# Self attention's queries and keys made block by block in one pipeline with the linear attention's norm

## The chip, the cores and the metric

One core of one Trainium2 chip runs the whole program. The metric is the device time of one execution in microseconds (us), lower is better. Engines: PE (TensorE), DVE (VectorE), ACT (ScalarE), POOL (GpSimd), SP (SyncE, which only issues DMAs here).

## The reference

Two transformer blocks over 1024 tokens of width 1024, batch 1, float32. The change lies in the first third of the first block, its two mixers, which read the same projected input:

```python
h = rms_norm(x, norm_mix)
c_q, c_kv, k_rope, hq, hf_fwd, hf_bwd, hi, hg = split_columns(h @ w_in)   # 192, 128, 32, 5 x 512
# self attention (MLA): 8 heads, q and k 64 + 32 wide, v 64 wide
q = (rms_norm(c_q, q_a_norm) @ w_q_up).reshape(B, S, 8, 96)
kv = (rms_norm(c_kv, kv_a_norm) @ w_kv_up).reshape(B, S, 8, 128)
k = concat([kv[..., :64], broadcast(k_rope)]); v = kv[..., 64:]
q, k = rms_norm(q, q_norm), rms_norm(k, k_norm)         # over 96, each head
q, k = [concat([t[..., :64], apply_rope(t[..., 64:], cos, sin)]) for t in (q, k)]
a = softmax(q @ k.T * 96 ** -0.5) @ v
# linear attention (HGRN2): 4 heads of 128, both directions
o = direction(hf_fwd) + direction(hf_bwd)
r = rms_norm(o, o_norm) * silu(hg)
x = x + concat([a, r]) @ w_out
```

Cross attention and an expert layer end the first block; a state space mixer and an MLP make the second.

## The kernel before

The kernel is written engine by engine. A stage is a `Block` in which each engine has its own instruction list, in the written order; semaphores carry the dependencies, and at the end of a block all engines meet. `c.chain` makes each of an engine's instructions wait for the one before it. Tokens lie in 8 blocks of 128 (`NT`), a block on the 128 partitions.

`mix_first` (L1188) runs the stages of the mixers:

- `norm_split` normalises and transposes the input. In the same block SP fetches small parameters (L1239).
- `project` (L364 to L509) is the product with `w_in`: 6 jobs of 8 weight pieces; for each piece ACT and DVE cut the weights into a high and a low part (L420, L424) and PE makes three products for each of 8 PSUM banks. Three cut pieces can stand ready. ACT evacuates job 0 into `mla_in` (c_q, c_kv, k_rope), job 1 with Silu, jobs 2 and 3 with two Sigmoids a bank.
- `hgrn` is the linear attention; its result goes to `mixed`, half of `mix_hT`.
- `group_norm` (L860 to L866), a product with the gate (L1270) and `turn` (L588) give `r` transposed.
- `mla`: `rope_tables` loads the positions and makes sine and cosine; `load` fetches weights and gains (L170); two `group_norm`s treat c_q and c_kv; a `turn` transposes them with the gains in its evacuation (L1377 to L1382); a block multiplies them up (L1400 to L1428), with PSUM for two token blocks at a time (`mla_up_ps`, 4 banks each); `mla_norms` normalises q and k in 8 parts, ACT squares, DVE sums and scales, POOL applies the gain (L1472 to L1501); `rope` rotates q on DVE and k on POOL (L1512 to L1515); two `turn`s transpose q and k (64 transposes of 96 x 128 each, copied out by ACT L593 and DVE L597).
- `head_pairs` is the attention: 64 units of 128 queries of a head; the row maximum gives the bias of the exponential (L807), whose scale is the constant `96 ** -0.5` (L830).

Each of these stages is its own block, so the stages do not overlap.

Of the kernel before, what the change touches and what calls it, by code (L numbers as in the profile page):

```python
# [17 lines left out]
P = 128  # L18
# [8 lines left out]
T = 1024  # L27
# [692 lines left out]
def head_pairs(c, name, qT, kT, v, room, mixT, scale):  # L720
# [15 lines left out]
    with ExitStack() as ctx:  # L736
# [19 lines left out]
        with nc.Block() as block:  # L756
# [68 lines left out]
            def _(act):  # L825
                def exps(i):
                    act.wait_ge(bias_ready, i + 1)
# [138 lines left out]
def hgrn(c, inputs, q, keep, key, values, lb, lb1, mask, queries, out):  # L966
# [11 lines left out]
    with ExitStack() as ctx:  # L978
        s = lambda n, shape: sbuf(ctx, nc, f"hg_{n}", shape)
        whole = s("whole", [P, 2, 2, T // 2])  # L980
        mine, pairT = s("mine", [P, 2, T]), s("pairT", [P, 2, NT, P])
        kdT, state = s("kdT", [P, 2, NT, P]), s("state", [P, 2, NT, P])
# [203 lines left out]

def mix_first(c, a, x):
    nc = c.nc  # L1188
    with ExitStack() as ctx:
        s = lambda n, shape, dt=F32: sbuf(ctx, nc, n, shape, dt)  # L1190
        hT, high = twins(ctx, nc, "mix_hT", "mix_high", [P, KD, T])
        mla_in = s("mla_in", [P, NT, QR + KVR + ROPE])
        w_in = a["w_in"][0].rearrange("(k p) n -> p k n", p=P)
        with ExitStack() as hg:
            s = lambda n, shape, dt=F32: sbuf(hg, nc, n, shape, dt)
            q = s("hg_q", [P, HH, T])
# [4 lines left out]
            key = s("hg_key", [P, 2, HH, T])  # L1201
# [16 lines left out]
            low = sbuf(low_, nc, "mix_low", [P, KD, T])  # L1218
# [6 lines left out]
            with low_:  # L1225
# [7 lines left out]
                small += [(onorm[:, 0], a["hg_o_norm"][0].unsqueeze(0).to_broadcast([P, HK]))]  # L1233
                small_in = c.hold_sem("hg_parameters_in")
# [10 lines left out]
                project(c, "mix_in", stream, jobs)  # L1245
# [15 lines left out]
            mixed = hT[:, 4:8].rearrange("p k t -> p (k t)").rearrange("p (m v) -> p m v", v=HH * HK)  # L1261
            hgrn(c, a, q, logf, key, values, lb, lb1, mask, queries, mixed)
            ssq = s("hg_ssq", [P, NT * HH])
            heads = lambda t: t.rearrange("p m (h v) -> p (m h) v", v=HK)
            group_norm(c, "hg_norm", heads(mixed), heads(values[:]), ssq[:], HK, onorm[:])
            with nc.Block() as block:
                @block.vector
                def _(dve):
                    do = c.chain("vector", dve)
                    do(nc.vector.tensor_tensor(values[:], mixed, gate[:], ALU.mult))  # L1270
            items = [[values[:, m, h * P:(h + 1) * P] for h in range(HH)] for m in range(NT)]
            turn(c, "hg_turn", items, lambda n, ps, copy: copy(
                hT[:, HH:, n * P:(n + 1) * P], ps.rearrange("p (h t) -> p h t", t=P)))
        mla(c, a, mla_in, hT, x[:].rearrange("p m d -> p (m d)"))
# [29 lines left out]


def rope_tables(c, ctx, a):

    nc = c.nc
    s = lambda n, shape, dt=F32: sbuf(ctx, nc, n, shape, dt)
    cos, sin = s("rope_cos", [P, NT, HALF]), s("rope_sin", [P, NT, HALF])  # L1310
    with ExitStack() as tmp:
        s = lambda n, shape, dt=F32: sbuf(tmp, nc, n, shape, dt)
        wide = a["positions"].dtype != I32
        posi = s("rope_posi", [P, NT, 2 if wide else 1], I32)
        pos, ang, t = s("rope_pos", [P, NT]), s("rope_ang", [P, NT, HALF]), s("rope_tmp", [P, NT, HALF])
        src = a["positions"][0]
        if wide:
            src = src.bitcast(I32)
        load(c, [(posi[:], src.rearrange("(m p two) -> p m two", p=P, two=2 if wide else 1))])
        with nc.Block() as block:  # L1320
            @block.vector
            def _(dve):
                do = c.chain("vector", dve)
                do(nc.vector.tensor_copy(pos[:], posi[:, :, 0]))
                for j in range(HALF):
                    freq = float(np.float32(1.0) / np.float32(ROPE_BASE ** (j / HALF)))
                    do(nc.vector.tensor_scalar(ang[:, :, j], pos[:], freq, None, ALU.mult))
                reduce_angle(nc, do, ang[:], t[:])

                do(nc.vector.tensor_scalar(t[:], ang[:], -1.0, None, ALU.mult))  # L1330
                do(nc.vector.tensor_tensor(t[:], t[:], ang[:], ALU.min))
                do(nc.vector.tensor_scalar(t[:], t[:], math.pi / 2, None, ALU.add))
        with nc.Block() as block:
            @block.scalar
            def _(act):
                nc.scalar.activation(sin[:], ang[:], ACT.Sin)
                nc.scalar.activation(cos[:], t[:], ACT.Sin)
    return cos, sin


def mla(c, a, mla_in, mixT, x):

# [1743 lines left out]
```

## Time and profile before

| | |
|---|---|
| three runs | median 3866.33 us (3858.35 to 3868.52) |
| the profiled execution | 3865.7 us, of it the profile's span 3864.0 us |
| PE busy | 3165.1 us, 82% of the span |
| DVE, ACT, POOL busy | 1470.3 (38%), 898.7 (23%), 175.4 us (5%) |
| mean granted PE clock | 0.904 of full speed |

In the page the span is cut into 40 slices of 96.6 us; the digits are the busy tenths of an engine in a slice, and PEclk the granted clock of PE in tenths (10 is printed as 9). The stages touched here are slices 5 to 7 of the lines below, from some 483 us to 773 us.

```profile
PE   7995732898869696477777279899999889999998
DVE  3116857776251432411111374652122433332334
ACT  3224311444141423000000113102132132111221
POOL 0000004000000000011111030000000000000000
PEclk9997966999989896689899689999999989999999
```

### The profile page before, as it was taken

Reading aid. Unit: us, or ns where it says so; the run is one execution under the profiler, and the core shown is the slowest. Engines: PE = TensorE matmul, PEld = TensorE weight load, DVE = VectorE, ACT = ScalarE, POOL = GpSimd, SP = SyncE. Lnnn points to the kernel's source line nnn. Section 1 sums busy time; section 2 is a strip of 40 time slices with the busy share of each in tenths; the row PEclk is TensorE's granted clock in tenths of the full one; section 3 lists DMA queues with packets and bytes.
Section 4 is the critical chain, followed back from the end, with each engine's and each line's share of the span. In section 5 each row is a group of like instructions: output and inputs, shape, how many; then the busy total and the mean of one; then the engine's idle time right before and its main releaser. Section 6 shows DMA issues by size and latency. Waiting matters only on the chain. (4 is left out here: it accounts for less than half of the span.)

```text
span 3864.0 us, 35977 instructions
## 1 busy us (share of the span) xinstructions
PE 3165.1 (82%) x14454; PEld 2342.5 (61%) x14454; DVE 1470.3 (38%) x2130; ACT 898.7 (23%) x1397; POOL 175.4 (5%) x220
## 2 busy tenths in 40 slices
PE   7995732898869696477777279899999889999998
PEld 7875721544657575222222168788877768888886
DVE  3116857776251432411111374652122433332334
ACT  3224311444141423000000113102132132111221
POOL 0000004000000000011111030000000000000000
PEclk9997966999989896689899689999999989999999
DMA  2110000001121014399999502211111211111111
GB/s 90 49 36 9 1 13 0 1 1 60 63 87 33 12 33 178 121 393 398 398 400 392 185 25 63 58 64 49 41 39 52 82 44 47 47 49 50 49 49 71
DMA packets 138439, 370.35 MB, mean 96 GB/s; under 512 B 44896, under 2 KB 59104, under 8 KB 112160
## 3 DMA queue, kind: packets, MB, share of 16 engines
q1 hardware_dynamic: 129072, 351.45, 25.4%
q0 software_dynamic: 9216, 16.80, 1.2%
q8 instruction: 106, 1.74, 0.2%
q14 instruction: 45, 0.37, 0.0%
HBM read 352.99 MB, written 32.79 MB: 100 GB/s over the span
## 5 line engine op out<-in xcount | busy, mean ns | idle before, releaser
L1873 PE MATMUL moe_ph<-moe_wgu,moe_rowsT 128*64 128x512 f32 x1024 | 264.1, 675 | 82.6 <-DMA moe_wgu<-in_moe_w_up_dram 43.6
L509 PE MATMUL mlp_ps<-mlp_high,mlp_w_cut 128*128 128x512 f32 x1024 | 317.1, 391 | 6.0 <-DVE mlp_w_cut L424 6.0
L509 PE MATMUL mlp_ps<-mlp_w_cut,mlp_hidden_high 128*128 128x512 f32 x1024 | 315.2, 389 | 0.0
L424 DVE TENSOR_TENSOR m_w_cut<-m_w_raw,m_w_cut 128x512 fp32r<-128x512 f32 (+1 forms) x92 | 94.3, 1029 | 453.4 <-ACT m_w_cut L420 453.1
L1873 PEld LDWEIGHTS moe_ph<-moe_wgu,moe_rowsT 128*64 128x64 f32 x1024 | 83.2, 155 | 243.5 <-issue 190.6
L424 DVE TENSOR_TENSOR mlp_w_cut<-mlp_w_raw,mlp_w_cut 128x1024 fp32r<-128x1024 f32 x64 | 78.3, 1225 | 398.9 <-ACT mlp_w_cut L420 398.4
L509 PEld LDWEIGHTS mlp_ps<-mlp_high,mlp_w_cut 128*128 128x128 f32 x1024 | 193.2, 189 | 46.6 <-DVE mlp_w_cut L424 6.4
L420 ACT ACTIVATE m_w_cut<-m_w_raw 128x512 fp32r<-128x512 f32 (+1 forms) x92 | 76.4, 835 | 604.3 <-PE m_gates_ps L509 196.4
L509 PEld LDWEIGHTS mlp_ps<-mlp_w_cut,mlp_hidden_high 128*128 128x128 f32 x1024 | 192.2, 188 | 39.9
L509 PE MATMUL mlp_ps<-mlp_low,mlp_w_cut 128*128 128x512 f32 x512 | 199.9, 390 | 0.0
L509 PE MATMUL mlp_ps<-mlp_w_cut,mlp_hidden_low 128*128 128x512 f32 x512 | 199.2, 389 | 0.0
L420 ACT ACTIVATE mlp_w_cut<-mlp_w_raw 128x1024 fp32r<-128x1024 f32 x64 | 67.6, 1058 | 528.1 <-PE mlp_ps L509 525.6
L509 PE MATMUL m_cv_ps<-m_high,m_w_cut 128*128 128x512 f32 x512 | 166.6, 408 | 25.1 <-DVE m_w_cut L424 15.9
L509 PE MATMUL m_gates_ps<-m_high,m_w_cut 128*128 128x512 f32 x512 | 160.9, 396 | 4.1 <-DVE m_w_cut L424 4.1
L1894 PE MATMUL moe_py<-moe_wd,moe_hidT 128*64 128x512 f32 x512 | 116.9, 598 | 29.0 <-DVE moe_hidT L1915 28.2
L1909 DVE TENSOR_TENSOR moe_hid<-moe_ph,moe_gated 128x256 f32<-128x256 f32 x32 | 13.6, 424 | 315.3 <-PE moe_pu L1881 290.2
L509 PEld LDWEIGHTS m_cv_ps<-m_high,m_w_cut 128*128 128x128 f32 x512 | 98.7, 196 | 48.8 <-DVE m_w_cut L424 17.0
L764 PE MATMUL mla_attn_scores<-mla_kT,mla_qT 96*128 96x512 f32 x256 | 121.7, 599 | 1.0 <-PEq L580 1.0
L509 PE MATMUL mix_in_ps<-mix_high,mix_w_cut 128*128 128x512 f32 x384 | 119.3, 392 | 0.0
L509 PE MATMUL mix_in_ps<-mix_w_cut,mix_high 128*128 128x512 f32 (+1 forms) x384 | 112.6, 374 | 3.7 <-DVE mix_w_cut L424 3.7
L1299 DVE TENSOR_TENSOR x<-mlp_ps,x 128x512 f32<-128x512 f32 x128 | 86.9, 689 | 72.3 <-PE mlp_ps L509 72.3
L509 PEld LDWEIGHTS m_gates_ps<-m_high,m_w_cut 128*128 128x128 f32 x512 | 96.8, 189 | 25.5 <-DVE m_w_cut L424 4.5
(530 smaller groups left out, 6006.3 us busy)
## 6 DMA issues: line engine op xcount, KB each, us to landing
moe_wgu<-in_moe_w_gate_dram SPq DMA_DIRECT2D x64, 1024.0 KB, 13.9
moe_wgu<-in_moe_w_up_dram SPq DMA_DIRECT2D x64, 1024.0 KB, 16.0
moe_wd<-in_moe_w_down_dram SPq DMA_DIRECT2D x64, 1024.0 KB, 9.5
mlp_w_raw<-in_w_ff_dram SPq DMA_DIRECT2D x64, 512.0 KB, 3.5
m_w_raw<-in_w_in_dram SPq DMA_DIRECT2D x48, 256.0 KB, 2.8
mix_w_raw<-in_w_in_dram SPq DMA_DIRECT2D x40, 256.0 KB, 2.6
m_w_raw<-in_w_in_dram SPq DMA_DIRECT2D x20, 512.0 KB, 3.7
x_w_raw<-in_x_w_kv_dram SPq DMA_DIRECT2D x16, 512.0 KB, 3.6
```

The costliest lines, as they stand in the source:

```text
L420: nc.scalar.activation(part(s, 0).bitcast(F32R), raw(s), ACT.Copy).then_inc(high_ready, 1)
L424: nc.vector.tensor_tensor(part(s, 1).bitcast(F32R), raw(s), part(s, 0), ALU.subtract).then_inc(low_ready, 1)
L509: ins = nc.tensor.matmul(ps[:, b, :r.shape[-1]], l, r, start=(k == 0 and sw is high and wh == 0), stop=(k == job.nk - 1 and sw is low))
L764: ins = nc.tensor.matmul(ps_s[i % 2][:, s], qT[:, h, m * P:(m + 1) * P], kT[:, h, s * CH:(s + 1) * CH], start=True, stop=True)
L1299: return nc.vector.tensor_tensor(x[:, b, at], ps, x[:, b, at], ALU.add)
L1873: ins = self.nc.tensor.matmul(self.ps_h[r, w].rearrange("p (i n) -> p i n", i=2), self.rowsT[:, w, k, r], self.wgu[:, w * self.parts + h, ...
L1894: ins = self.nc.tensor.matmul(self.ps_y[r, half], self.hidT[:, w, k, r], self.wd[:, w * self.parts + h, k, half * CH:(half + 1) * CH], sta ...
L1909: self.nc.vector.tensor_tensor(self.hid[:, b % self.small], self.ps_h[:, b % self.small, EH:], self.gated[:, b % self.small], ALU.mult).th ...
```

## The change

The linear attention's norm and everything between it and `head_pairs` become one block, `mla_prepare`. It goes through the token blocks in one loop: transposing c_q and c_kv, the two products, the norms, the rotation, the transposes of q, k and r, all interleaved. Other parts:

- The row norms of c_q and c_kv, and the sine and cosine tables, are made by a `Side` that runs within `project` of `w_in`: 24 ACT squares with a sum, three for each of pieces 16 to 23, then two square roots, a sine and a cosine; on DVE the angles, and the rotation of k_rope once for all heads.
- q and k are scaled by their row norms as they leave PSUM. The gains of q and k on the first 64 columns are multiplied together and applied to k alone, as it leaves its transpose (L1542); the gain on the last 32 goes into the rotation's tables.
- q's own norm is not applied to q. Its reciprocal `rq` (with `96 ** -0.5` in it) is the per-partition scale of the exponential and goes into its bias.
- The gain of the linear attention's norm is multiplied into the gate on POOL; POOL also rotates q.
- PSUM: two banks for q, two for k and v (one token block at a time), four as a ring for all transposes, in the order of `ring`.
- Small parameters are fetched in `norm_split`'s block (8 DMAs more); the three weight matrices at the start of `mla_prepare`. The working buffers of `hgrn` and the low part of the projection lie in the room of `mla_qT`, `mla_kT` and `mla_v`. `hgrn` writes its result over `values`.

Attention:

```diff
-                    nc.vector.tensor_scalar(bias[:, i:i + 1], top[:, i:i + 1], -scale, None,
-                                            ALU.mult).then_inc(bias_ready, 1)
+                    h, m = place(i)
+                    nc.vector.tensor_scalar(bias[:, i:i + 1], top[:, i:i + 1], rq[:, h, m:m + 1], -1.0,
+                                            ALU.mult, ALU.mult).then_inc(bias_ready, 1)
...
                     nc.scalar.activation(probs[:, i % 2].rearrange("p (s k) -> p s k", k=CH), ps_s[i % 2][:],
-                                         ACT.Exp, bias=bias[:, i:i + 1], scale=scale,
+                                         ACT.Exp, bias=bias[:, i:i + 1], scale=rq[:, h, m:m + 1],
```

The calls in `mix_first` (`group_norm`, the product, `turn` and `mla` go):

```diff
-                project(c, "mix_in", stream, jobs)
+                rope = RopeTables(c, mla_in, posi[:, :, 0], cos[:], sin[:], kn[:], scales[:], (qg[:], kg[:]),
+                                  gate[:].rearrange("p m v -> p (m v)"))
+                project(c, "mix_in", stream, jobs, side=rope)
...
-            hgrn(c, a, q, logf, key, values, lb, lb1, mask, queries, mixed)
+            hgrn(c, a, q, logf, key, values, lb, lb1, mask, queries, values, lies)
+            mla_prepare(c, a, mla_in[:], rope, qn[:], (qga[:], qgb[:], kvg[:]), onorm[:], values[:], gate[:], hT,
+                        x[:].rearrange("p m d -> p (m d)"), qT[:], kT[:], v[:], rq[:])
```

The core of `mla_prepare`, the ring, PE and DVE:

```diff
+    ring = [("low", 0)]
+    for i in range(NT + 1):
+        ring += [("low", i + 1)] if i + 1 < NT else []
+        ring += [(n, i - 1, j) for n in "kq" for j in range(2)] if i else []
+        ring += [("hg", i)] if i < NT else []
...
+                def turn_into(item, parts):
+                    n = place[item]
+                    if n >= 4:
+                        pe.wait_ge(freed[n % 4], n // 4)
...
+                for i in range(NT + 1):
+                    if i < NT:
+                        is_free(pe, ("low", i))
+                        w = lowT[i % 2]
+                        if i:
+                            pe.wait_ge(q_copied, i)
+                            pe.wait_ge(q_squared, i)
+                        for b in range(2):
+                            nc.tensor.matmul(ps_q[:, b, :hq], w[:, 0], wqa[:, b * hq:(b + 1) * hq],
+                                             start=True, stop=False)
+                            ins = nc.tensor.matmul(ps_q[:, b, :hq], w[:QR - P, 1], wqb[:, b * hq:(b + 1) * hq],
+                                                   start=False, stop=True)
+                        ins.then_inc(q_made, 1)
+                        if i:
+                            pe.wait_ge(v_taken, i)
+                            pe.wait_ge(k_scaled, i)
+                        for b in range(2):
+                            ins = nc.tensor.matmul(ps_kv[:, b], w[:, 2], wkv[:, b * CH:(b + 1) * CH],
+                                                   start=True, stop=True)
+                        ins.then_inc(kv_made, 1)
+                    if i + 1 < NT:
+                        low(i + 1)
+                    if i:
+                        pe.wait_ge(k_ready, i)
+                        for j in range(2):
+                            turn_into(("k", i - 1, j), [k[(i - 1) % 2][:, 4 * j + h] for h in range(4)])
+                        pe.wait_ge(q_roped, i)
+                        for j in range(2):
+                            turn_into(("q", i - 1, j), [q[(i - 1) % 2][:, 4 * j + h] for h in range(4)])
+                    if i < NT:
+                        pe.wait_ge(hg_ready, i + 1)
+                        turn_into(("hg", i), [values[:, i, h * HK:(h + 1) * HK] for h in range(HH)])
...
+                for i in range(NT + 1):
+                    if i < NT:
+                        dve.wait_ge(k_squared, i + 1)
+                        nc.vector.tensor_reduce(rk[:, i], k_sq[i % 2], AX, ALU.add).then_inc(k_summed, 1)
+                        if i + 1 < NT:
+                            hg_sum(i + 1)
...
+                        nc.vector.tensor_tensor(k[i % 2][:, :, 0:NOPE], kv[:, :, 0:NOPE], wide(factor[:, i], NOPE),
+                                                ALU.mult).then_inc(k_scaled, 1)
...
+                        if i + 1 < NT:
+                            take_low(i + 1)
+                        dve.wait_ge(q_squared, i + 1)
+                        nc.vector.tensor_reduce(rq[:, :, i], q_sq[i % 2], AX, ALU.add).then_inc(q_summed, 1)
+                    if i:
+                        for j in range(2):
+                            ps, sem = bank(("k", i - 1, j), dve)
+                            nc.vector.tensor_scalar(kT[:, 4 * j:4 * j + 4, (i - 1) * P:i * P],
+                                                    ps[:QK].rearrange("p (h t) -> p h t", t=P), side.gain[:QK],
+                                                    None, ALU.mult).then_inc(sem, 1)
+                    if i + 1 < NT:
+                        hg_norm(i + 1)
```

ACT copies q out, squares k's part and q from PSUM, copies v, makes the three square roots of a block and takes the banks of q and r. On POOL a block is six products of 128 x 128 for the rotation, then one of 128 x 512 for the gate.

**Order on PE.** Before, the products of the token blocks stand one behind another, and wait for PSUM only two blocks back (`mla_up_ps`, L1400 to L1405, blocks 1 to 3):

```order
L1400 MATMUL mla_up_ps<-mla_wqa,mla_cqT 128x384
L1402 MATMUL mla_up_ps<-mla_wqb,mla_cqT 128x384
L1400 MATMUL mla_up_ps<-mla_wqa,mla_cqT 128x384
L1402 MATMUL mla_up_ps<-mla_wqb,mla_cqT 128x384
L1405 MATMUL mla_up_ps<-mla_wkv,mla_ckvT 128x512 x2
L1400 MATMUL mla_up_ps<-mla_wqa,mla_cqT 128x384 [waits mla_kv_taken_66,mla_q_taken_65]
```

In the change, token block 2 of `mla_prepare`, from its first product to the next block's (rows that wait for nothing are left out; `prep_t` is the ring of four banks, `x` the scratch room that holds q, k and the transposed c_q and c_kv):

```order
L1404 MATMUL prep_q<-prep_wqa,x 128x384 [waits prep_q_squared_61,prep_q_copied_60,prep_bank3_freed_74]
L1413 MATMUL prep_kv<-prep_wkv,x 128x512 [waits prep_k_scaled_58,prep_v_taken_65]
L1388 MATMUL prep_t<-ident,mla_in 128x128 [waits prep_bank1_freed_72]
L1388 MATMUL prep_t<-ident,x 96x128 [waits prep_bank2_freed_73,prep_k_ready_59]
L1388 MATMUL prep_t<-ident,x 96x128 [waits prep_bank3_freed_74]
L1388 MATMUL prep_t<-ident,x 96x128 [waits prep_bank0_freed_71,prep_q_roped_64]
L1388 MATMUL prep_t<-ident,x 96x128 [waits prep_bank1_freed_72]
L1388 MATMUL prep_t<-ident,hg_values 128x128 [waits prep_bank2_freed_73,prep_hg_ready_69]
L1404 MATMUL prep_q<-prep_wqa,x 128x384 [waits prep_q_squared_61,prep_q_copied_60,prep_bank1_freed_72]
```

The products of a block now stand behind five turns, each of which waits for a bank of the ring: the second turn of q for the bank that c_q and c_kv of this same block held, the turn of r for the bank that k's first turn of this same block holds.

**Order on DVE.** In `mla_prepare`, one token block, from the sum of k's squares to the next (`mla_rq` takes the sum of q's squares):

```order
L1520 TENSOR_REDUCE prep_rk<-x 128x8 [waits prep_k_squared_55]
L1500 TENSOR_REDUCE prep_hg_r<-x 128x4 [waits prep_hg_squared_66]
L1524 RECIPROCAL prep_rk<-prep_rk 128x8 [waits prep_k_rooted_57]
L1525 TENSOR_SCALAR prep_factor<-prep_rk,mla_scales 128x8 [waits vector_step]
L1532 TENSOR_TENSOR x<-mla_in,prep_rk 128x8x32
L1494 TENSOR_SCALAR x<-prep_t,mla_qga 128x128 [waits prep_turned_50]
L1495 TENSOR_SCALAR x<-prep_t,mla_qgb 64x128
L1496 TENSOR_SCALAR x<-prep_t,mla_kvg 128x128
L1538 TENSOR_REDUCE mla_rq<-x 128x8 [waits prep_q_squared_61]
L1542 TENSOR_SCALAR mla_kT<-prep_t,mla_qg 96x4x128 [waits prep_turned_50] x2
L1504 RECIPROCAL prep_hg_r<-prep_hg_r 128x4 [waits prep_hg_rooted_68]
```

(Between the fourth and the fifth row stands the scaling of k's part out of PSUM, L1530.) The rows that free c_q's bank (L1496) and k's (the first of L1542) come late in it.

**Order on ACT**, in `project`: around the evacuation of job 2 (`x` and `hg_key` are the two Sigmoids of a bank, 8 pairs, of which one stands here). The last rows:

```order
L420 ACTIVATE mix_w_cut<-mix_w_raw 128x512
L1257 ACTIVATE hg_gate,mla_scales<-mla_in 128x192
L1257 ACTIVATE hg_gate,mla_scales<-mla_in 128x128
L1257 ACTIVATE hg_gate,mla_scales<-mla_in 128x32
L1617 ACT_TABLE_LOAD
L1617 ACTIVATE x<-mix_in_ps 128x512
L1618 ACTIVATE hg_key<-mix_in_ps 128x512
L420 ACTIVATE mix_w_cut<-mix_w_raw 128x512
L1266 ACT_TABLE_LOAD
L1266 ACTIVATE mla_scales<-mla_scales,eps 128x8 x2
L1269 ACT_TABLE_LOAD
```

Three squares have come between the last cut and the evacuation, and three loads of function tables are new: two behind the evacuation of job 2, one ahead of that of job 3.

## Rows read from the trace of the kernel before

**Rows 1.** Windows: us; busy (count) of PE, PEld, DVE, ACT, POOL; PEclk, DMA, GB/s
```profile
497.00:528.50 31.50, 6.05 (x32) 5.84 (x32) 25.23 (x10) 4.12 (x7) 0.00 (x0) 0.57 0.00 0
528.50:548.50 20.00, 0.00 (x0) 0.00 (x0) 5.26 (x26) 1.79 (x3) 0.00 (x0) 0.53 0.24 61
548.50:566.00 17.50, 4.88 (x25) 4.45 (x26) 12.69 (x20) 5.36 (x15) 0.00 (x0) 0.56 0.00 0
566.00:608.40 42.40, 40.77 (x96) 15.33 (x96) 11.91 (x24) 6.48 (x8) 0.00 (x0) 1.00 0.00 1
608.40:655.00 46.60, 0.00 (x0) 0.00 (x0) 40.93 (x24) 13.54 (x16) 27.39 (x8) 0.54 0.00 0
655.00:679.00 24.00, 0.00 (x0) 0.01 (x1) 22.82 (x48) 0.00 (x0) 22.03 (x48) 0.50 0.00 0
697.40:940.00 242.60, 234.23 (x993) 108.34 (x994) 187.27 (x320) 112.55 (x199) 0.00 (x0) 0.99 0.00 1
```
**Rows 2.** Timeline at both ends: start, us, engine, line, instruction [idle before, releaser]
```profile
497.43 4.42 DVE L860 TENSOR_TENSOR hg_values<-mix_hT 128x4096 f32<-128x4096 f32 x1 [8.62 <-PEq L1021]
...
697.54 3.67 PE L764 MATMUL mla_attn_scores<-mla_kT,mla_qT 96*128 96x512 f32 x8 [1.04 <-PEq L580]
```
**Rows 3.** Timeline of the products, first two token blocks
```profile
565.90 0.88 PE L1400 MATMUL mla_up_ps<-mla_wqa,mla_cqT 128*128 128x384 f32 x2 [1.29 <-PEq L580]
...
571.25 0.81 ACT L1414 ACTIVATE x<-mla_up_ps 128x768 f32<-128x768 f32 x1 [6.07 <-PE mla_up_ps L1405]
...
576.33 0.81 ACT L1414 ACTIVATE x<-mla_up_ps 128x768 f32<-128x768 f32 x1 [4.27 <-PE mla_up_ps L1405]
```
**Rows 4.** Timeline, the nearest rows to the new instructions
```profile
552.49 0.20 DVE L863 RECIPROCAL mla_ssq<-mla_ssq 128x8 f32<-128x8 f32 x1 [0.37 <-ACT mla_ssq L871]
...
561.65 0.33 DVE L1378 TENSOR_SCALAR mla_cqT<-mla_turn_ps,mla_qgb 64x128 f32<-64x128 f32 x1
...
615.40 1.75 DVE L1486 TENSOR_REDUCE mla_norm_ssq<-mix_hT 128x16 f32<-128x1536 f32 x1
...
689.33 7.16 PE L588 MATMUL mla_k_turn_ps<-ident,mla_k 128*96 128x128 f32 x64 [1.05 <-PEq L580]
...
692.60 0.59 ACT L593 ACTIVATE mla_kT<-mla_k_turn_ps 96x512 f32<-96x512 f32 x1 [0.28 <-PE mla_k_turn_ps L588]
...
693.04 0.69 DVE L597 COPY mla_kT<-mla_k_turn_ps 96x512 f32<-96x512 f32 x1 [0.19 <-PE mla_k_turn_ps L588]
```
**Rows 5.** Timeline, POOL beside DVE
```profile
615.57 3.43 POOL L1501 TENSOR_TENSOR x<-x,mla_qn 128x1536 f32<-128x1536 f32 x1 [321.12 <-DVE x L1494]
...
617.34 3.27 DVE L1494 TENSOR_TENSOR x<-x,mla_norm_ssq 128x1536 f32<-128x1536 f32 x1
...
655.13 0.46 POOL L1512 TENSOR_TENSOR mix_hT<-mla_k,rope_cos 128x128 f32<-128x128 f32 x1 [0.32 <-ACTq L1438]
```
**Rows 6.** Timeline, PE within the linear attention
```profile
379.20 0.49 PE L1177 MATMUL hg_ps<-hg_values,hg_pairT 128*128 128x128 f32 x2 [2.21 <-DVE hg_state L1120]
379.53 1.02 PE L1180 MATMUL hg_ps<-hg_state,mix_hT 128*128 128x128 f32 x4
...
383.16 0.61 PE L1180 MATMUL hg_ps<-hg_state,mix_hT 128*128 128x128 f32 x4
...
408.50 1.94 PE L1164 MATMUL hg_ps<-ident,hg_key 128*128 128x128 f32 x16 [2.35 <-issue]
```
**Rows 7.** The tile of the last weight matrix: its issue (ns) and landing
```profile
L170 SPq DMA_DIRECT2D mla_wkv<-in_mla_w_kv_up_dram x1: 586/586/586, 542.6 to 542.6; - x1
DMA to landing us min/median/max: 4.7/4.7/4.7
```
**Rows 8.** Timeline, ACT's table load; SP's small parameters, next issue
```profile
150.60 1.28 ACT L1212 ACT_TABLE_LOAD   x1
...
14.30 1.86 SPq L1239 DMA_DIRECT2D hg_onorm<-in_hg_o_norm_dram  x1
34.55 22.79 SPq L364 DMA_DIRECT2D mix_w_raw<-in_w_in_dram  x8
```

More of the change, by code:

```diff
@@ L717, in _, with head_pairs @@
                         copy_bank(act, lambda o, t: nc.scalar.activation(o, t, ACT.Copy), i - 1, 0)
[L720 removed]
+def head_pairs(c, name, qT, kT, v, room, mixT, rq):
     nc = c.nc
@@ L963, in view, with hgrn @@
     return bass.AP(tensor=a.tensor, offset=a.offset + offset, ap=[list(a.ap[0])] + [list(d) for d in dims])
-def hgrn(c, inputs, q, keep, key, values, lb, lb1, mask, queries, out):
+def hgrn(c, inputs, q, keep, key, values, lb, lb1, mask, queries, out, lies):
     nc = c.nc
@@ L1184, in _, with turn, vector, scalar @@
                 over_steps(step)
+class Side:
+    banks, ps, piece = 0, None, 0
+    def turn(self, steps, s, share):
+        self.piece = 10 ** 6 if s is None else s
+        left = 10 ** 6 if s is None else share
+        while left > 0:
+            cost = next(steps, None)
+            if cost is None:
+                break
+            left -= cost
+    def vector(self, dve, s):
+        pass
+    def scalar(self, act, s):
+        pass
+    def tensor(self, pe, s):
+        pass
+    def sync(self, sp, s):
+        pass
+    def gpsimd(self, pool):
+        pass
@@ L1217, in mix_first @@
             low_ = ExitStack()
-            low = sbuf(low_, nc, "mix_low", [P, KD, T])
+            low = lies("mix_low", [P, KD, T], 48)
             pair = (high, low)
@@ L1260, in mix_first @@
             queries = hT[:, 0:4].rearrange("p (a d) t -> p a d t", a=2)
-            mixed = hT[:, 4:8].rearrange("p k t -> p (k t)").rearrange("p (m v) -> p m v", v=HH * HK)
-            hgrn(c, a, q, logf, key, values, lb, lb1, mask, queries, mixed)
[L1263 to L1274, printed above, removed]
+            hgrn(c, a, q, logf, key, values, lb, lb1, mask, queries, values, lies)
+            mla_prepare(c, a, mla_in[:], rope, qn[:], (qga[:], qgb[:], kvg[:]), onorm[:], values[:], gate[:], hT,
+                        x[:].rearrange("p m d -> p (m d)"), qT[:], kT[:], v[:], rq[:])
+        head_pairs(c, "mla_attn", qT, kT, v,
+                   x[:].rearrange("p m d -> p (m d)").rearrange("p (j e q) -> p j e q", e=2, q=CH), hT, rq)
+        own.close()
         with ExitStack() as w_:
@@ L1303, in add_jobs @@
     return [Job(columns(w, i), True, src, add(i), "vector") for i in range(D // CH)]
[L1306 to L1338, printed above, removed]
@@ L2271, in output_factors @@
         return self.power(slice(0, SJ + 1), SJ + 1), c_wide
-class Side:
-    banks, ps, piece = 0, None, 0
-    def turn(self, steps, s, share):
-        self.piece = 10 ** 6 if s is None else s
-        left = 10 ** 6 if s is None else share
-        while left > 0:
-            cost = next(steps, None)
-            if cost is None:
-                break
-            left -= cost
-    def vector(self, dve, s):
-        pass
-    def scalar(self, act, s):
-        pass
-    def tensor(self, pe, s):
-        pass
-    def sync(self, sp, s):
-        pass
-    def gpsimd(self, pool):
-        pass
 class Convolution(Side):
```

440 lines of the change are left out of this document (282 added, 158 removed).

## The prediction

> **What bounds the kernel now.** I read the windows by stage first, then the timeline at their ends, then single rows as prices. Between the linear attention's last copy and self attention's first product the stages stand one behind another [rows 1]: a norm that is DVE alone (25.23 of 31.5 us), a stretch of DMA and tables in which nothing works for long, row norms, the products (PE 40.77 of 42.4 us), the norms of q and k (DVE 40.93 of 46.6 us, PE idle), the rotation (DVE 22.82 and POOL 22.03 of 24 us), and the transposes. The reader is to see that in each window one engine is full and the others empty. The stretch runs from 497.43 to 697.54, **200.1 us** [rows 2]. The attention behind it is paced by PE, 234.23 of 242.6 us busy [rows 1].
>
> **The new block, round by round.** I did not add up busy times. I walked through the instruction lists of the five engines with durations from the rows. The prices:
> - From the first product of a token block to the copy of q: 5.35 us; block to block 5.08 us [rows 3], so q's and k's products take 5.08 us of PE and 0.27 until ACT runs. q's four are 3.36 of it (four times 384 of 2560 columns).
> - A turn of four: 7.16 us for 64, so 0.44 [rows 4].
> - ACT on 512 columns 0.59, on 768 0.81 [rows 3, 4]. DVE on 512 columns out of PSUM 0.69; a sum 1.75 for 1536 columns, so about 0.69 for 512 and 0.96 for 768; a small reciprocal 0.20, a copy of 128 columns 0.33 [rows 4]. Independent instructions follow each other some 0.07 before the full duration.
> - POOL 0.46 for 128 columns, 3.43 for 1536, so 1.2 for the gate's 512 [rows 5].
>
> If the engines ran freely side by side, a round would cost the fullest of them: PE 5.08 + 23 transposes of 0.11 = 7.6 us, DVE about 7.2. It does not come out so. PE's list puts the turn of r ahead of the next block's products, and that turn needs the bank of k's first turn, which DVE frees late. So the loop closes through both engines:
>
> products to the result 5.35; ACT squares k 0.6; then DVE in a row: sum of k 0.62, sum of r 0.62, reciprocal and factor 0.42, scaling k 0.62, its last 32 columns 0.36, three copies of c_q and c_kv 0.80, sum of q 0.89, first copy of k's transpose 0.69 (5.0 together); the turn of r 0.44; three crossings of 0.03. Sum **11.5 us a round**. ACT's and POOL's work (6 and 4 us a round) lies beside it, as do k's root, the second copy of k and the linear attention's norm (1.2 us).
>
> The whole block: weights 6.2 us (two issues of 0.6 ahead of the last, 4.7 to landing [rows 7], 0.3 to start); first round 13.1 (9.5, and 3.6 because PE starts at half clock after idling); six rounds of 11.5, 68.8; the last from its products to the copies of q, 13.3; 0.4 to the attention. **101.8 us**.
>
> PE's clock is the doubtful term. In a round PE waits 2.8 us between q's first and second turn, for the bank that c_q held. In the linear attention a wait of 2.21 us was followed by matmuls at 1.2 GHz (four take 1.02 against 0.61) for some 3.6 us; another wait, of 2.35, was followed by full rate, 16 in 1.94 us [rows 6]. So rounds will go both ways. A low stretch of 3.6 us doubles the turn of r (0.44) and costs about 0.8 of the next product. I take 1.2 in six rounds, **7 us**; the ends are 0 and 2.5 a round, 15 us.
>
> **Other edits.** Within the projection ACT gets three squares for each of eight pieces, 0.6 at most each (a 512-column row is 0.59 [rows 4]), and three table loads of 1.28 [rows 8]. A piece takes PE far longer and three cut pieces are in stock, so they are covered, except at the end of job 2, where three squares stand ahead of an evacuation that already had a table load. I take **1 us**, between 0 and 4.5 (three squares and a load, with a load at the next job's end). If the stock were gone, all of it would lie open (a rival below). DVE's small work there is 16 and some instructions, hidden the same way.
> SP gets eight more small fetches. The last of the old ones went out at 14.3 to 16.2, and SP issues nothing until 34.55 [rows 8]; eight of at most 1.86 end at 31. Nothing; if they ended later, the projection would start later by as much, 2 us at most.
> `hgrn` writes elsewhere and its buffers lie elsewhere: no instruction more, nothing. The wait behind it: its PSUM and semaphores are used as before.
> Attention: the scale is read per partition, the bias gets a second operand. No row shows an exponential with such a scale. ACT is busy 112.55 of 242.6 us there and DVE 187.27, PE sets the pace [rows 1], so I take nothing. The ends are -2 and +6 (0.1 in each of 64 units, were the cover gone). PE comes to it out of a thin stretch, perhaps at half clock: **1 us**.
>
> Sum: -200.1 + 101.8 + 7 + 1 + 1 = -89.3. The profiled execution took 3865.7 us, 0.6 under the median: 3776.4, and by the median **3777 us**.
>
> **The rivals.**
> - *PE at half clock throughout.* PE's waits in each round keep it at 1.2 GHz: products 5.1 and a turn 0.4 longer, a round 17 us, the block 143. Time 3865.7 - 200.1 + 143 + 2 = 3811. For it: the 2.8 us wait in every round, and the low stretch behind a shorter one [rows 6]. Against: the same rows show the clock back after about 3.6 us of work, and 5 us of products stand in each round. The Trainium skill, "TensorE: Matmul & The Clock Gate", section "A second HAM failure mode: psum-queue depth-cycling", speaks against this change: a kernel that cycles through PSUM banks, with PE idling briefly between groups, swings between both levels and pays at each return. The trace agrees in that both levels occur in one stage.
> - *POOL holds DVE up.* While POOL ran its 3.43 us, DVE's product of two SBUF operands took 3.27 us and ended 1.6 behind POOL, whereas the sum at 615.40 took its 1.75 undisturbed [rows 4, 5]. In the new round the last 32 columns of k and the norm of r are such products. In my walk POOL is done 0.3 us before the first comes; if it is late by all its work (six of 0.46 and 1.2, 4.0 us), a round is 15.5 and the time 3809. The Trainium skill, "SBUF — State Buffer", section "Who interferes with whom", has this as an exclusive lock of the pair of ports, with the loser blocked for the whole instruction; the trace agrees.
> - *The ring does not bind.* If DVE frees the banks in time, the round is PE's, 7.8 us, the block 77: 3744. For it: DVE's and PE's busy sums; against: the written order.
> - *The side work is not hidden* and the change does not do what it says: 24 squares of 0.59, three loads, four small ones lie open, 19 us: 3796.
> - *Slower than before.* The engines work in lockstep and PE at half clock: PE 15.2 + DVE 7.6 + ACT 6 + POOL 4 = 33 us a round, the block 270, time 3936. It decides from 23.7 us a round (200.1 less 10, by eight). For it: each engine waits for another at some 25 places a round; against: only the chain above is a loop.
>
> **How the numbers follow.** Forecast 0.68, half clock 0.10, POOL 0.10, ring free 0.06, side work 0.03, slower 0.03. The forecast alone spans 3764 (no low stretch, no cold start, nothing added) to 3792. To leave out no more than 2 in 10 the range must reach POOL's and half clock's cases: 3761 to 3812; it leaves out the free ring and the slower one. A measurement of this kernel tells 0.3%, 12 us, from no change; every case but the last is beyond it: faster 0.96, same 0.01, slower 0.03.
>
> **What would show it.** In the trace after: from the linear attention's last copy to the first L764-like product about 110 us; PE's q products 11.5 to 12.7 us apart; the turn of r released by DVE's copy into `mla_kT`; ahead of it a wait of nearly 3 us for `take_low`. POOL's products not overlapping DVE's scaling of k. The projection as long as before within 2 us, the attention within 5 of its 242. Wrong if rounds are under 9 or over 15 us, if q's products take 6.7 us in most rounds, or if the time moves outside this stretch.

## The result and the profile after

The change took **3805.38 us** (median of 4 runs, 3802.60 to 3807.06) against 3862.57 for the kernel before, run beside it (4 runs, 3858.35 to 3868.52): ratio 0.9849, 95% interval 0.9836 to 0.9862, so 57 us faster. The forecast was 3777 within 3761 to 3812. The sign and the place were right, and a third of the gain did not come. The time lies in the stated range only because that was drawn out to the cases of the rivals; the forecast by itself ended at 3792. The profiled execution took 3802.6 us, its span 3800.8, the mean granted PE clock 0.911. It is the fastest of the four, so the trace is 26.2 us past the 3776.4 that I had worked out for a profiled execution, and the median 28 past 3777.

The page after, to be laid beside the lines of before:

```profile
PE   7995767998766885777777389899999879999998
DVE  3125845783242514111110573642223333333334
ACT  3324334442233411000000213002132132112211
POOL 0000011000000000111110030000000000000000
PEclk9996878999878995898898599999999989999999
```

Slices are 95.0 us now. The new block lies in slices 5 and 6 (counted from 0), where POOL shows its 1s; the attention fills what were norms and rotations before.

Windows of the change: the new block with the first units' start, and the attention. Then the block cut at the first, second and last product of q and at the attention's first. Columns as in [rows 1].

```profile
501.30:632.20 130.90, 93.89 (x280) 44.70 (x280) 58.20 (x142) 49.19 (x91) 30.43 (x56) 0.74 0.03 9
632.20:872.00 239.80, 230.50 (x980) 106.34 (x980) 188.70 (x317) 117.25 (x197) 0.00 (x0) 1.00 0.00 1
...
502.60:508.15 5.55, 0.52 (x3) 0.31 (x3) 4.26 (x13) 2.73 (x4) 2.49 (x2) 0.65 0.66 202
508.15:522.45 14.30, 10.76 (x20) 4.09 (x20) 3.47 (x10) 3.44 (x6) 3.80 (x7) 0.62 0.00 0
522.45:613.43 90.98, 68.17 (x211) 33.08 (x211) 42.82 (x104) 35.19 (x67) 21.58 (x41) 0.76 0.00 0
613.43:632.24 18.81, 14.44 (x51) 7.25 (x49) 7.65 (x18) 6.84 (x13) 2.57 (x6) 0.73 0.00 1
```

The block takes 129.6 us where the stages took 200.1 [rows 2]; I had given it 108.8, its clock term of 7 included. The excess of 20.8 is, part by part: weights 5.55 for 6.2 (-0.7), first round 14.3 for 13.1 (+1.2), **six rounds 90.98 for 75.8 (+15.2)**, the last 18.81 for 13.7 (+5.1). PE is busy 68.17 of the 90.98 us, far more than six times my 7.6: its instructions are long, at a granted clock of 0.76.

PE's timeline, one round at full clock and the start of the next (start, us, engine, line, instruction [idle before, releaser]):

```profile
554.87 0.81 PE L1404 MATMUL prep_q<-prep_wqa,x 128*128 128x384 f32 x2
555.61 0.91 PE L1406 MATMUL prep_q<-prep_wqb,x 64*128 64x384 f32 x2
...
558.13 1.98 PE L1413 MATMUL prep_kv<-prep_wkv,x 128*128 128x512 f32 x4
559.95 0.49 PE L1388 MATMUL prep_t<-ident,mla_in 128*128 128x128 f32 x3
560.28 1.47 PE L1388 MATMUL prep_t<-ident,x 128*96 128x128 f32 x12
565.01 0.64 PE L1388 MATMUL prep_t<-ident,x 128*96 128x128 f32 x4 [3.25 <-DVE x L1496]
566.61 1.09 PE L1388 MATMUL prep_t<-ident,hg_values 128*128 128x128 f32 x4 [0.97 <-DVE mla_kT L1542]
567.49 1.49 PE L1404 MATMUL prep_q<-prep_wqa,x 128*128 128x384 f32 x2
568.91 1.65 PE L1406 MATMUL prep_q<-prep_wqb,x 64*128 64x384 f32 x2
...
572.06 1.65 PE L1406 MATMUL prep_q<-prep_wqb,x 64*128 64x384 f32 x2
573.64 3.12 PE L1413 MATMUL prep_kv<-prep_wkv,x 128*128 128x512 f32 x4
```

The reader is to see three things. The two waits stand where the prediction put them, with the releasers that it named (the copy of c_q's bank, the copy of k's first turn). Behind them PE is at 1.2 GHz: a pair of q's products takes 1.65 us in place of 0.91, and the four of k and v 3.12 in place of 1.98. And that is most of a product phase, not its first 0.8 us. q's first products start at 508.15, 522.45, 538.57, 554.87, 567.49, 583.44, 597.38 and 613.43; of the eight rounds only that of 554.87 has all its products at full rate.

The rest of the time: the linear attention's first table load came at 305.87 for 301.55 before, its last copy at 501.32 for 496.10. From the attention's first product to the start of its last copy out it was 249.97 us for 249.57. So of the 26.2 us by which the trace misses the sum, the block has 20.8 and what lies ahead of it 4.2 (5.2 for 1); the attention took 0.6 less than its term of 1, and some 1.8 lie in later stages, where nothing was looked for.

### The profile page after: what moved, and what is told of

Same layout as the page of the kernel before. It is cut to its first block and busy times, and to the rows that moved or that the text cites. A ratio compares the mean times of both kernels' runs of the same rounds, so it can differ in the third digit from the quotient of the medians.

```text
span 3800.8 us, 35996 instructions
## 1 busy us (share of the span) xinstructions
PE 3191.7 (84%) x14454; PEld 2341.5 (62%) x14454; DVE 1410.2 (37%) x2144; ACT 925.5 (24%) x1477; POOL 156.6 (4%) x220
## 5 line engine op out<-in xcount | busy, mean ns | idle before, releaser
L509 PE MATMUL mlp_ps<-mlp_low,mlp_w_cut 128*128 128x512 f32 x512 | 200.1, 391 | 0.0
```

Of the source, the lines that this page charges most:

```text
L509: ins = nc.tensor.matmul(ps[:, b, :r.shape[-1]], l, r, start=(k == 0 and sw is high and wh == 0), stop=(k == job.nk - 1 and sw is low))
```

## The experiments

The theory: what is missing in the block is PE's clock, which each round's wait of 2.5 to 3.3 us in one piece takes away; the chain itself is as predicted. Rivals: a longer chain, POOL beside DVE, the ring's order. In each comparison the kernel before ran beside the experiment, between 3863 and 3865 us.

**Dummy work in PE's wait.**

```diff
                         for j in range(2):
+                            at = place["q", i - 1, j]
+                            pe.wait_ge(freed[at % 4], at // 4)
+                            for _ in range((20, 6)[j] if i < NT else 0):
+                                nc.tensor.transpose(ps_t[:, at % 4, 0:P], c.ident[:], c.ident[:])
                             turn_into(("q", i - 1, j), [q[(i - 1) % 2][:, 4 * j + h] for h in range(4)])
```

> The changed kernel with idle PE time in mla_prepare filled: in each of rounds 1 to 7, 20 transposes of the identity ahead of q's first turn (into the bank that this turn then overwrites) and 6 ahead of the second. Nothing else moves. Theory A (the 2.5 to 3.3 us for which PE waits in each round let its clock fall to 1.2 GHz, and the products behind run at half rate): the products' rows at 0.81 to 0.91 us for two instead of 1.65, granted clock near 1.00 from the second round on, rounds of 12 us instead of 12.6 to 16.3, the block some 107 us instead of 129.6, time 3783 us. Rival B (the round is set by DVE's and ACT's chain, the clock is a symptom that costs little): rounds as before or up to 1 us longer for the added work, time 3805 to 3812.

Measured 3777.07 us (3774.94 to 3780.44), ratio 0.9778 (0.9762 to 0.9795). A round's waiting turn of q and the next products, PE's timeline:

```profile
555.53 2.35 PE L1427 MATMUL prep_t<-ident 128*128 128x128 f32 x20
557.72 0.60 PE L1388 MATMUL prep_t<-ident,x 128*96 128x128 f32 x4
559.41 0.87 PE L1427 MATMUL prep_t<-ident 128*128 128x128 f32 x6 [1.09 <-DVE x L1500]
560.12 0.60 PE L1388 MATMUL prep_t<-ident,x 128*96 128x128 f32 x4
561.02 0.63 PE L1388 MATMUL prep_t<-ident,hg_values 128*128 128x128 f32 x4 [0.30 <-DVE mla_kT L1546]
561.48 0.81 PE L1404 MATMUL prep_q<-prep_wqa,x 128*128 128x384 f32 x2
```

26 useless transposes a round buy 28 us by the medians. In the two traces the block is 18.9 us shorter (129.6 to 110.7) and the executions lie 22.2 apart; what makes up the rest of the 28 is not shown. The second round is still at half rate (16.03 us), behind a wait of 3.53 us in the first, which has no dummies. From the third on every product runs at full rate, the granted clock is 1.00, and the rounds take 12.24 us or less, but for the last of 14.20. The other work, the ring and the chain are those of the change, so the clock term is what was missing in the rounds. What is left of a wait, 1.09 us, did not cost the clock.

**A round lengthened: q's own norm applied to q after all** (DVE takes a reciprocal and a product of 768 columns per block; not shown are PE's wait for `q_scaled` ahead of q's turns, and the constant that now stands in `rq`).

```diff
+                        dve.wait_ge(q_rooted, i + 1)
+                        do(nc.vector.reciprocal(rq[:, :, i], rq[:, :, i]))
+                        dve.wait_ge(q_roped, i + 1)
+                        nc.vector.tensor_tensor(q[i % 2], q[i % 2], wide(rq[:, :, i], QK), ALU.mult).then_inc(q_scaled, 1)
```

> The changed kernel with q's own norm applied to q again in mla_prepare: behind the sum of q's squares DVE waits for the root and the rotation, takes the reciprocal and multiplies q (768 columns); PE waits for that ahead of q's turns; the exponential's scale is a column of the constant. It prices the title's second half. Theory A (DVE's work ahead of k's first copy lies on the loop): 1.5 us more a round (0.3 root, 0.2 reciprocal, 0.9 product, crossings), time 3817 to 3823. Rival B (it fits beside PE's products, which run at half rate): under 0.3 us a round, time 3805 to 3808.

Measured 3822.59 us (3820.86 to 3825.72), ratio 0.9897 (0.9880 to 0.9913); rounds of 18.6 us. Two rows of DVE and one of PE:

```profile
555.90 0.96 DVE L1543 TENSOR_TENSOR x<-x,mla_rq 128x768 f32<-128x768 f32 x1
556.78 1.40 DVE L1547 TENSOR_SCALAR mla_kT<-prep_t,mla_qg 96x512 f32<-96x512 f32 x2
...
557.67 1.08 PE L1389 MATMUL prep_t<-ident,hg_values 128*128 128x128 f32 x4 [2.86 <-DVE mla_kT L1547]
```

DVE's added stretch, its wait of 0.70 us for ACT's root included, puts k's first copy 1.89 us later behind the sum of q's squares, and it lands one for one in PE's wait for that copy (2.86 us in place of 0.97): the loop is closed where the prediction closed it. Moving q's norm into the exponential's scale is worth 17 us in this version. Not all of that is the longer chain: here every round has half rate products, in the change not, and the granted clock from 522 to 614 us is 0.65.

**The turn of r ahead of k's and q's** (on PE, in the ring and on ACT; the ring is shown).

```diff
         ring += [("low", i + 1)] if i + 1 < NT else []
-        ring += [(n, i - 1, j) for n in "kq" for j in range(2)] if i else []
         ring += [("hg", i)] if i < NT else []
+        ring += [(n, i - 1, j) for n in "kq" for j in range(2)] if i else []
```

> Only the turn of r is moved ahead of k's and q's turns, on PE, in the ring and on ACT; DVE's row stays. The bank of k's first turn is then out of the loop; PE's next products wait behind q's turns, which wait for the bank of c_q and c_kv: 5.35 + 0.6 + DVE 3.44 (sum of k, sum of r, reciprocal and factor, scaling, last columns, three copies) + 0.9 for q's turns + crossings = 10.4 us a round at full clock, with a wait of about 2.3 us left in one piece. Theory A (such a wait drops the clock): half rate products in most rounds, 12.5 to 14.5 us a round, time 3785 to 3798. Rival B (the ring's order alone is the whole gain of both moves, clock kept): rounds 10.4, time 3762 to 3772. Rival C (the loop was never closed through the turn of r): rounds as in the change, 3800 to 3808.

Measured 3784.08 us (3780.73 to 3791.13), ratio 0.9795 (0.9778 to 0.9813). PE's timeline:

```profile
569.15 1.05 PE L1388 MATMUL prep_t<-ident,x 128*96 128x128 f32 x8 [3.34 <-DVE x L1497]
570.03 0.81 PE L1404 MATMUL prep_q<-prep_wqa,x 128*128 128x384 f32 x2
...
580.26 1.05 PE L1388 MATMUL prep_t<-ident,x 128*96 128x128 f32 x8 [3.34 <-DVE x L1497]
581.14 1.25 PE L1404 MATMUL prep_q<-prep_wqa,x 128*128 128x384 f32 x2
```

The round at full clock is 11.1 us (I had worked out 10.4), others 14 to 16: shorter chain, same clock trouble. These two waits are both of 3.34 us, and only behind the second were the products slow, so the wait's length alone does not decide. The block takes 113.9 us (498.08 to 612.01) for the change's 129.6. Time just under the expected 3785.

**DVE's three copies early, the ring as in the change** (`take_low` right behind the sum of r's squares).

```diff
                         if i + 1 < NT:
                             hg_sum(i + 1)
+                            take_low(i + 1)
...
-                        if i + 1 < NT:
-                            take_low(i + 1)
```

> Only DVE's three copies of c_q and c_kv are moved, to right behind the sum of r's squares; the ring stays as in the change. By my walk the loop is the same length (11.5 us a round: the first copy of k's transpose still ends DVE's row), but PE's one wait of 2.7 to 3.3 us is split: about 1.1 ahead of q's second turn, about 2.5 ahead of the turn of r. Theory A (a wait of 2.5 us drops PE's clock just as 3.2 does, and it now stands right ahead of q's products): the products stay at half rate in most rounds, rounds 13 to 16 us, time within 10 us of the change's, 3795 to 3810. Rival B (what counts is the idle time in one piece of 3 us or more, and the split is enough): q's products at 0.81 to 0.91, rounds 11.5 to 12.2, time 3772 to 3780. Rival C (the early copies alone are what made the version with both moves fast, since they shorten the loop): rounds near 10, time under 3768.

Measured 3797.02 us (3794.65 to 3798.76), ratio 0.9823 (0.9808 to 0.9839).

```profile
577.89 0.64 PE L1388 MATMUL prep_t<-ident,x 128*96 128x128 f32 x4 [1.22 <-DVE x L1496]
580.93 0.63 PE L1388 MATMUL prep_t<-ident,hg_values 128*128 128x128 f32 x4 [2.40 <-DVE mla_kT L1541]
581.39 1.20 PE L1404 MATMUL prep_q<-prep_wqa,x 128*128 128x384 f32 x2
```

The wait is split into 1.22 and 2.40 us, as expected, and nothing is won by that: the first round is shorter (12.59 us), five of the six behind it take 16 us and one 11.61, and the block is 129.5 us (498.40 to 627.88) as in the change. Its median is 8 us lower than the change's, but in its trace the linear attention ended 4 us earlier, which this edit does not touch, and the intervals of the two ratios overlap.

**Both moves together.**

> The changed kernel with two moves in mla_prepare: the turn of r ahead of k's and q's turns (in the ring, on PE and on ACT), and DVE's three copies of c_q and c_kv right behind the sum of r's squares. Both waits of PE for a bank of the ring go. Theory A (PE's waits on the ring make the round, by themselves and by the clock): the loop is then products 5.4, ACT's square 0.7, sum 0.7, root 0.3, q's square 0.9, so rounds of 8 to 9 us, clock 1.00, the block 86 to 92 us, time 3762 to 3769 us. Rival B (DVE's chain sets the round whatever PE does): rounds of 11 to 12 us, time 3785. Rival C (the clock is low for another reason, such as short bursts of transposes): products stay at 1.65 us for two, rounds of 12 to 13, time 3790.

Measured 3762.13 us (3760.49 to 3766.99), ratio 0.9744 (0.9727 to 0.9760).

```profile
567.67 1.05 PE L1388 MATMUL prep_t<-ident,x 128*96 128x128 f32 x8 [1.31 <-DVE x L1497]
568.55 0.81 PE L1404 MATMUL prep_q<-prep_wqa,x 128*128 128x384 f32 x2
```

From the third round on one wait of 1.31 us a round is left, the granted clock is 1.00, and the round is 9.08 us. Against the change this is 43 us, where the moves alone gave 21 and 8. In the traces the six rounds fall from 90.98 to 59.02 us. Of these 32 us, 15 are the shorter chain at full clock (11.61 to 9.08, six times); the others are the clock, with the 1.2 of the POOL experiment below. The turn of r ahead alone left a wait of 3.34 us, the early copies alone one of 2.40, and in both half rate rounds stayed; only together do they make it short.

**The start of the tiles.** In the projection a piece of jobs 1 to 3 took 5.60 us in the change and 5.49 before. By the layout of the compiled programs, as I read it, the raw and the cut weights start at a multiple of 64 bytes before and 32 bytes past one in the change, where `mla_scales` (3 x 8 floats, 96 bytes) lies ahead of them; no trace shows addresses, and what the experiment tests is a shift by 32 bytes.

```diff
-            scales = s("mla_scales", [P, 3, NT])
+            scales = s("mla_scales", [P, 4, NT])
```

> The changed kernel with mla_scales 32 bytes a partition longer (a row that nothing reads), so that the tiles laid behind it (hg_values, hg_gate, the raw and the cut weights of the projection) begin at a multiple of 64 bytes again, as in the kernel before. Theory A (the cut weights' start at 32 modulo 64 slows PE in jobs 1 to 3, where they are the stationary operand): a piece of jobs 1 to 3 takes 5.49 us again instead of 5.60, the projection ends 2.6 us earlier, time 3802 to 3803. Rival B (the squares and small work of the side, or the new place of mix_low, slow it): the pitch stays 5.60, time 3805.

Measured 3799.43 us (3794.51 to 3802.51), ratio 0.9837 (0.9821 to 0.9853). ACT's cuts at the pace of the pieces; the first fence is of the change, the second of this version:

```profile
85.08 0.63 ACT L420 ACTIVATE mix_w_cut<-mix_w_raw 128x512 fp32r<-128x512 f32 x1 [4.97 <-PE mix_in_ps L509]
90.69 0.63 ACT L420 ACTIVATE mix_w_cut<-mix_w_raw 128x512 fp32r<-128x512 f32 x1 [4.97 <-PE mix_in_ps L509]
```

```profile
84.83 0.63 ACT L420 ACTIVATE mix_w_cut<-mix_w_raw 128x512 fp32r<-128x512 f32 x1 [4.86 <-PE mix_in_ps L509]
90.33 0.63 ACT L420 ACTIVATE mix_w_cut<-mix_w_raw 128x512 fp32r<-128x512 f32 x1 [4.86 <-PE mix_in_ps L509]
```

The pitch is 5.49 to 5.50 again, and the linear attention's table load comes at 303.23 in place of 305.87. In the whole time that does not stand out (the intervals overlap); in the trace it does, and the three aligned versions agree (303.23, 303.17 and 302.98; the other six experiments and the change 304.68 to 306.18). Its block, on the other hand, took 133.3 us for the change's 129.6, with the same instructions: six rounds of 94.00 in place of 90.98, at a granted clock of 0.72 in place of 0.76. So how much of the block falls on half rate differs between executions of the same instructions, and in this trace that took back what the projection gave. Which of the tiles behind `mla_scales` it is was not tried.

**POOL's gate product out of DVE's way**, in the version with dummy transposes.

```diff
+                    if 0 < m < NT - 1:
+                        pool.wait_ge(hg_ready, m + 1)
+                        gate_gain(m + 1)
                     pool.wait_ge(q_copied, m + 1)
...
-                    if m + 2 < NT:
-                        gate_gain(m + 2)
```

> The version with dummy transposes (all rounds from the third on at full clock, 12.23 us each), and in it POOL's product of the gate moved from behind q's rotation to ahead of it, where DVE is done with the linear attention's norm and idle. In the version without this move the gate's product (1.28 us from 556.22) lay beside DVE's small product for the factor, which took 0.84 us there and 0.23 in the low clock rounds of the change. Theory A (the two contend, as my rival on POOL had it, and this is the part of it that came true): factor 0.23 to 0.25, rounds 11.5 to 11.7, the time 3 to 5 us less than 3777, so 3772 to 3774. Rival B (0.84 is a wait for something else): factor 0.84, rounds 12.2 as before, 3775 to 3779.

Measured 3777.65 us (3775.13 to 3781.12), ratio 0.9779 (0.9762 to 0.9795): the whole time does not show it. The rows do. Without the move, POOL's product and DVE's factor:

```profile
556.22 1.28 POOL L1561 TENSOR_TENSOR hg_gate<-hg_gate,hg_onorm 128x512 f32<-128x512 f32 x1
...
556.68 0.84 DVE L1529 TENSOR_SCALAR prep_factor<-prep_rk,mla_scales 128x8 f32<-128x8 f32 x1
```

and with it:

```profile
566.59 0.23 DVE L1529 TENSOR_SCALAR prep_factor<-prep_rk,mla_scales 128x8 f32<-128x8 f32 x1
```

DVE's small product had ended with POOL's. Undisturbed it takes 0.23 us, and the round 11.61 in place of 12.23. Four rounds had it, so the block is 2.5 us shorter (500.03 to 608.20, for 501.06 to 611.76). In the change itself it comes in two rounds (at 562.30 and 592.19, 0.82 us each). That is how much of the POOL rival came true: 1.2 us in the change, and none of it on the instructions that I had named. The Trainium skill, "SBUF — State Buffer", section "Who interferes with whom", lists `tensor_scalar`, in its two-port mode, among what can take the shared ports; the row agrees.

**A version beyond both kernels:** both moves, the aligned tiles, and 28 transposes of the identity while PE waits for the weights.

```diff
                 low(0)
+                for _ in range(28):
+                    nc.tensor.transpose(ps_t[:, 3, 0:P], c.ident[:], c.ident[:])
                 pe.wait_ge(w_in, 48)
```

> Both moves together, the scratch tile widened so that later tiles start at a multiple of 64 bytes, and 28 transposes of the identity (result used by nobody) while PE waits for the weights at the start of the block. Theory A (the three effects are apart and add): both moves 3762, alignment 3.6 to 4 less, and the first round at full instead of half clock (its q and kv products take 10.0 us instead of 5.1, of which 3 to 5 come back, less what 28 transposes run over the weights' landing): 3754, between 3751 and 3758; the first products at 0.81 to 0.91 each. Rival B (the start is bounded by other things, the clock there costs nothing): 3758 to 3760. Rival C (alignment paid only beside the change's own order): 3760 and more.

Measured 3746.39 us (3743.60 to 3754.64, 5 runs), ratio 0.9691 (0.9677 to 0.9705), 8 us better than the 3754 expected. The profiled execution was the slowest of the five, 3754.64, close to it; why the others are up to 11 us faster no trace shows.

```profile
499.19 3.22 PE L1396 MATMUL prep_t<-ident 128*128 128x128 f32 x28
504.23 0.91 PE L1406 MATMUL prep_q<-prep_wqa,x 128*128 128x384 f32 x2 [1.81 <-DMA prep_wkv<-in_mla_w_kv_up_dram]
```

The first round is at full clock now; the block takes 85.0 us (498.84 to 583.85). Then 18 more of these transposes behind the first turn of r:

> The best version so far (3746), and 18 more transposes of the identity in the first round, behind the turn of r, where PE waits 2.10 us for c_q's copies and then makes two of q's four products and those of k and v at half clock (round 12.45 us instead of 9.08). Theory A (the one wait drops the clock): q's products of the second round all at 0.81 to 0.91, kv 1.98, that round 9.1 to 9.4, time 3 us less, 3743. Rival B (the clock falls there for what PE did before, dummies or not): round 12, time as before, 3746.

Measured 3744.57 us (3742.53 to 3748.10), ratio 0.9692 (0.9676 to 0.9709), no difference that the whole time could show. In the trace the second round is 9.18 us for 12.45 before, as expected:

```profile
507.42 2.13 PE L1424 MATMUL prep_t<-ident 128*128 128x128 f32 x18
509.68 0.91 PE L1406 MATMUL prep_q<-prep_wqa,x 128*128 128x384 f32 x2
...
518.86 0.81 PE L1406 MATMUL prep_q<-prep_wqa,x 128*128 128x384 f32 x2
```

## Why the prediction came out as it did

**The chain: right.** I gave a round 11.5 us at full clock. With the clock kept and POOL out of the way it is 11.61 (the gate experiment). The terms, from start to start: sum of k 0.61 for 0.62, sum of r 0.59 for 0.62, factor and reciprocal 0.49 for 0.42, copies 0.78 for 0.80. One price beside the sum was wrong: four times 384 of 2560 columns are 3.05 of 5.08 us, not 3.36 (measured 3.26), and twice that was my 6.7 us for q's products at half clock, which took 6.1 to 6.3. The waits and releasers are as named, and adding to DVE's row added to the round.

**The clock term: the step that failed.** It said "A low stretch of 3.6 us doubles the turn of r (0.44) and costs about 0.8 of the next product. I take 1.2 in six rounds, 7 us; the ends are 0 and 2.5 a round, 15 us." Measured: six rounds 90.98 us, less six of 11.61 (69.7) and 1.2 for POOL, is 20.1, so **3.3 us a round**, past my upper end; in the aligned version, with one round of POOL's 0.6, it is 4.0. The round at 567.49 shows how: q's products 6.15 us (to 573.64) where the dummy version has 3.26 (549.25 to 552.51), those of k and v 2.95 for 1.82, the turn of r 0.4 more. The low clock lasted from the turn of r at 566.61 until well into k's and v's products, 7 us or more, not 3.6. I had read the length of the low stretch from one place of the linear attention [rows 6] and took it for a constant. Even at that length the price was too low: 3.6 us at half rate lose up to 1.8, and I charged 1.2. The number of low stretches was not the error. The text said that rounds would go both ways, but the sum charged one in each of the six, and one of the eight rounds had all its products at full rate.

By the signs that I had set, this part was wrong although the time is in the range: q's products 11.5 to 12.7 us apart came once, four of the six rounds took more than 15 us (15.95 to 16.30), and in five of the eight q's products were at half rate from the first to the last, in a sixth all but (1.41 us for the first pair in place of 1.49).

The same holds for the ends. In the first round I had counted 3.6 us for half clock, and all its products were at it (14.3 us for 13.1); to the last round I gave nothing, and it took 18.81 us, for 14.2 in the gate experiment: 4.6 of the 5.1 by which I missed it.

**The rival on half clock** (3811) stood nearer to 3805 than the forecast. The rule beside it, from the Trainium skill, "TensorE: Matmul & The Clock Gate", section "A second HAM failure mode: psum-queue depth-cycling", described what happened: a swing between both levels, paid at each return. Its chance of 0.10 was too small for a wait that stood in every round.

**Ahead of the block: 1 us forecast, 5.2 measured.** Of it 4.3 lie in the projection (the linear attention's table load). The alignment experiment gives back 2.6 of that; so "its buffers lie elsewhere: no instruction more, nothing" was false for the projection, whose cut weights had moved too, and which I had not costed at all. Of the 1.7 left, 0.9 come at the end of job 2 (in the aligned version ACT's cuts run 0.8 us behind those of before ahead of it, 150.77 for 149.95, and 1.7 behind it, 179.12 for 177.44), where I had put 1 us for the squares and table loads. The 0.8 ahead of it stand in the first pieces, and no cause is shown for them. The other 0.9 is within what the linear attention varies by itself: from its table load to its last copy it took 195.5 us in the change and 191.5 and 191.6 in two experiments that do not touch it.

**The parts costed at nothing.** SP's eight more fetches went out from 16.20 to 20.4 and the next weights at 34.77, for 34.55 before [rows 8]: right. The attention: its exponential grew by 0.09 us each, DVE's bias by 0.06, and the stretch by 0.4 us in all, since PE paces it: right. Column by column (busy us, mean ns, idle before), the change:

```profile
L833 ACT ACTIVATE mla_attn_probs<-mla_attn_scores,mla_attn_bias,mla_rq 128x1024 f32<-128x1024 f32 x64 | 77.1, 1205 | 122.6 <-DVE mla_attn_bias L809 122.6
```

and before:

```profile
L830 ACT ACTIVATE mla_attn_probs<-mla_attn_scores,mla_attn_bias 128x1024 f32<-128x1024 f32 x64 | 71.3, 1114 | 128.1 <-DVE mla_attn_bias L807 128.1
```

**The other rivals.** The side work was hidden but for the end of job 2. The ring did bind: with it loosened the round fell to 9.08 us. Lockstep did not come.

## What to carry to other kernels

- When stages are fused into a pipeline round, cost the critical engine's waits twice: once as time, and once as PE's clock behind them. Here waits of 2.5 to 3.3 us in rounds of 11.6 cost 3.3 us more a round on average, and less or more in a single one; one wait of 1.3 us cost nothing. Shorten the longest wait until the clock holds, or fill it with work that nobody reads.
- Two reorderings can be worth more together than the sum of both (here 21 and 8 us apart, 43 together), where one wait hides behind the other. Try them in one run as well as apart.
- After adding a small tile ahead of large ones, compare the pace of an untouched stage before and after.

## What was not expected of the hardware

- With the tiles behind `mla_scales` 32 bytes further on (by my reading from 32 past a multiple of 64 to a multiple) a piece of jobs 1 to 3 ran in 5.49 us in place of 5.60. Jobs 4 and 5 took 5.60 before and in the aligned version too, and 5.62 in the change; why is open.
- The same wait of 3.34 us, in successive rounds of the same length, was followed by full rate once and by half rate the next time. What decides between them no run here shows.
- A DVE product of 8 columns took 0.84 us beside POOL's 512, and 0.23 alone.
